# Another element order for the gate weights, and who makes the second one-hots and the score splits beside them

## What is computed

```python
def peer_ffn(h, w_q, keys, u_tab, v_tab):
    q = (h @ w_q).reshape(bsz, s, PK_HEADS, PK_DIM)
    s1 = einsum('bshd,hnd->bshn', q[..., :PK_HALF], keys[:, 0])
    s2 = einsum('bshd,hnd->bshn', q[..., PK_HALF:], keys[:, 1])
    v1, i1 = top_k(s1, 16)
    v2, i2 = top_k(s2, 16)
    cand = v1[..., :, None] + v2[..., None, :]
    best, c = top_k(cand, 16)
    e1 = take(i1, c // 16)
    e2 = take(i2, c % 16)
    expert = e1 * 128 + e2
    gate = softmax(best)
    # every token: 8 heads x 16 experts of 128 x 128
    act = gelu(einsum('tkd,td->tk', u_tab[expert], h))
    return einsum('tk,tkd->td', gate * act, v_tab[expert])
```

## Time and profile before

| | before |
|---|---|
| runs | 1711.5, 1711.54, 1712.85 us |
| median | 1711.54 us |
| the profiled execution | 1711.12 us |
| its span in the trace | 1709.3 us |
| PE busy | 1696.2 us, 99% of the span |
| DVE busy | 1393.0 us, 81% |
| ACT, POOL busy | 743.2 us, 664.6 us |
| granted TensorE clock | 1.00 of full (2.4 GHz) throughout |

### The profile page before, as it was taken

How to read it: one execution, slowest core, us unless ns; L and a number is a source line. 1 busy time by engine, 2 the same in 40 slices (tenths; PEclk the granted TensorE clock), 3 DMA queues, 4 the chain that set the end, 5 groups by cost and what they waited for, 6 DMA issues and landing times.

```text
span 1709.3 us, 33793 instructions
## 1 busy us (share of the span) xinstructions
PE 1696.2 (99%) x12021; PEld 1500.9 (88%) x12021; DVE 1393.0 (81%) x2763; ACT 743.2 (43%) x1060; POOL 664.6 (39%) x555
## 2 busy tenths in 40 slices
PE   9999999999999999999999999999999999999998
PEld 6878888788888999999998888888888888888887
DVE  5379989566688999999996998887778888777886
ACT  5555545543333333477774433333333333333333
POOL 0000000010253666788783554443334444343440
PEclk9999999999999999999999999999999999999999
DMA  5221122253322555566669999999999999999982
GB/s 184 87 75 40 49 95 79 87 195 121 122 76 74 169 173 175 179 237 249 234 231 352 391 394 392 330 331 342 345 366 345 345 337 332 334 356 356 352 309 97
DMA packets 158288, 399.07 MB, mean 233 GB/s; under 512 B 12512, under 2 KB 78176, under 8 KB 156416
## 3 DMA queue, kind: packets, MB, share of 16 engines
q1 hardware_dynamic: 118496, 252.20, 42.0%
q0 software_dynamic: 39712, 145.77, 22.8%
HBM read 353.75 MB, written 44.04 MB: 233 GB/s over the span
## 4 chain that ended last, share of the span: by engine, by line
PE 95%; DVE 2%; ACT 1%; DMA 1%; issue 0%; DVEq 0%; ACTq 0%
PE unit L426 95%; DMA g_dram<-ge 0%; DVE oneh L2121 0%; PE unit L578 0%; ACT L1164 0%; DVE rs L1654 0%; DMA xin<-xT 0%; DVE yo L2262 0%; ACT ld L1164 0%; DVE cy L1979 0%; ACT aa L1164 0%; ACT wH L1164 0%; DVE wL L1635 0%; ACT k L1164 0%; ACT best L1164 0%
## 5 line engine op out<-in xcount | busy, mean ns | idle before, releaser
L426 PE MATMUL unit<-h2H,uH 128*128 128x384 f32 x1024 | 348.9, 341 | 0.2 <-ACTq L1491 0.2
L426 PE MATMUL unit<-h2L,uH 128*128 128x384 f32 x1024 | 343.7, 336 | 0.0
L2324 POOL DMA_INDIRECT ring<-u_tab,idx x128 | 189.4, 1480 | 219.2 <-DVE accs L2198 192.3
L426 PE MATMUL unit<-vH,aH 128*128 128x512 f32 x768 | 237.9, 391 | 0.6 <-DVE aL L2173 0.5
L426 PE MATMUL unit<-vH,aL 128*128 128x512 f32 x768 | 237.2, 390 | 0.0
L426 PE MATMUL unit<-vL,aH 128*128 128x512 f32 x768 | 237.2, 390 | 0.0
L2324 POOL DMA_INDIRECT ring<-v_tab,idx x128 | 150.3, 1174 | 214.5 <-DVE ring L2184 208.2
L426 PE MATMUL unit<-h2H,uL 128*128 128x384 f32 x1024 | 204.0, 336 | 0.0
L1164 ACT ACTIVATE ge<-unit 128x384 f32<-128x384 f32 x128 | 62.4, 488 | 322.7 <-PE unit L426 322.7
L426 PEld LDWEIGHTS unit<-h2H,uH 128*128 128x128 f32 x1024 | 192.6, 188 | 2.8 <-issue 0.4
L426 PEld LDWEIGHTS unit<-h2L,uH 128*128 128x128 f32 x1024 | 192.5, 188 | 2.4
(11 more groups left out here) (316 smaller groups left out, 3204.5 us busy)
## 6 DMA issues: line engine op xcount, KB each, us to landing
uraw<-uT SPq DMA_DIRECT2D x128, 512.0 KB, 7.1
vraw<-v_tab SPq DMA_DIRECT2D x128, 512.0 KB, 8.6
wraw<-wall SPq DMA_DIRECT2D x68, 512.0 KB, 3.7
w_dram<-wst SPq DMA_DIRECT2D x12, 2048.0 KB, 6.7
wg<-w_dram SPq DMA_DIRECT2D x31, 768.0 KB, 9.7
g_dram<-ge SPq DMA_DIRECT2D x64, 192.0 KB, 1.9
gl<-g_dram SPq DMA_DIRECT2D x32, 384.0 KB, 11.6
gate_dram<-gst POOLq DMA_DIRECT2D x16, 256.0 KB, 2.3
```

The costliest lines, as they stand in the source:

```text
L426: return pe.matmul(out, lhsT, rhs, start=start, stop=stop, skip_group_check=True)
L2324: pool.indirect_dma_start(out=ring[k][:, :], out_offset=None, in_=(u_tab, v_tab)[half], in_offset=bass.IndirectOffsetOnAxis(ap=idx[:, SR * ...
```

## The change

Three edits.

1. The gate weights get another order of elements: `w_dram` is [group of four e1, partition, token, e1 in the group], and so are `wst` and `wg`. ACT's copy writes runs of four elements. A `wst` store goes out in runs of 512 bytes (32 tokens x 4 e1), 32 of them a partition. A `wg` load is one run of 6 KB a partition. `weigh` reads `wg` with a step of four elements.
2. POOL makes no one-hots. DVE makes the four `oh2` of a batch by one TENSOR_TENSOR of 128x512, the constant row (repeated four times) against the four tokens' values (each repeated 128 times). `e2s`, `oh2_ready`, `pool_order` and `batch_begun` are gone.
3. The stage's `u_low` (blocks 40 to 64) are POOL's, once per `j`. DVE's last `u_low` ahead of the main loop, of block 65, stays where it was, with a wait for POOL's.

```diff
-    e2s = at("e2s", 186.75, [P, 2 * T_W])
...
-    wst = at("wst", 125, [P, 2, NK, T_W])
+    wst = at("wst", 125, [P, 2, NG, T_W, G])
-    wg = at("wg", 157, [P, 2, NTB, G, T_W])
+    wg = at("wg", 157, [P, 2, TD, G])
...
                         batch = 16 * i + 4 * j + b
-                        pe.wait_ge(oh2_ready, batch + 1)
                         pe.wait_ge(rh_ready, batch + 1)
                         pe.wait_ge(wst_ready, batch + 1)
...
-                sp.dma_start(wg[:, par], w_dram[:, :, bass.ds(q * G, G), :].rearrange("b p e t -> p b e t")
-                             ).then_inc(wg_loaded[par], 16)
+                src = w_dram[q] if isinstance(q, int) else w_dram[bass.ds(q, 1)].rearrange("q p t e -> p (q t) e")
+                sp.dma_start(wg[:, par], src).then_inc(wg_loaded[par], 16)
...
-                        sp.dma_start(w_dram[bass.ds(2 * i + b, 1)].rearrange("b p e t -> p (b e) t"),
-                                     wst[:, b, :, :]).then_inc(wst_stored[b], 16)
+                        sp.dma_start(w_dram[:, :, bass.ds(2 * T_W * i + T_W * b, T_W), :].rearrange(
+                            "q p t e -> p q t e"), wst[:, b]).then_inc(wst_stored[b], 16)
...
-                    fn(wst[:, j // 2, :, o:o + 4].rearrange("p e t -> p t e"),
-                       bank[6 + b % 2][:, :].rearrange("p (t e) -> p t e", t=4), ACT.Copy).then_inc(wst_ready, 1)
+                    fn(wst[:, j // 2, :, o:o + 4, :].rearrange("p q t e -> p t q e"),
+                       bank[6 + b % 2][:, :].rearrange("p (t q e) -> p t q e", t=4, e=G), ACT.Copy).then_inc(wst_ready, 1)
...
-            dve.wait_ge(ul_ready, PRE_T)
-            u_low(PRE_T, 0)
...
                         for k in range(4):
                             tok = bass.ds(2 * T_W * i + 16 * j + 4 * b + k, 1)
-                            ins = tsc(rh[:, b, k, :], C(C_IOTA), et[:, 0, tok], et[:, 2, tok],
-                                      ALU.is_equal, ALU.mult)
-                            if k >= POOL_HOT:
-                                ins = tsc(oh2[:, b, k, :], C(C_IOTA), et[:, 1, tok], None, ALU.is_equal)
-                        ins.then_inc(rh_ready, 1)
-                        if b == 2:
-                            u_low(PRE_T + 4 * i + j + 1, (j + 1) % 4)
+                            tsc(rh[:, b, k, :], C(C_IOTA), et[:, 0, tok], et[:, 2, tok], ALU.is_equal, ALU.mult)
+                        four = et[:, 1, bass.ds(2 * T_W * i + 16 * j + 4 * b, 4)]
+                        tt(oh2[:, b, :, :], C(C_IOTA).unsqueeze(1).broadcast_to([P, 4, P]),
+                           four.unsqueeze(2).broadcast_to([P, 4, P]), ALU.is_equal).then_inc(rh_ready, 1)
...
-                tt(af[:, g % 2, :].rearrange("p (b t) -> p b t", t=T_W), src.rearrange("p (b t) -> p b t", t=T_W),
-                   wg[:, par, :, g, :], ALU.mult).then_inc(act_ready, 1)
+                tt(af[:, g % 2, :], src, wg[:, par, :, g], ALU.mult).then_inc(act_ready, 1)
...
+            dve.wait_ge(ul_ready, NPRE + 1)
             u_low(NPRE + 1, 1)
...
             with pool.Fori(0, PRE_T // 4) as i:
                 for j in range(4):
                     u_low(4 * i + j, j)
-            wait_taken(pool, "e2T")
+            u_low(PRE_T, 0)
             pool.wait_ge(idx_ready, 1)
...
-            for n in range(2):
-                hots(n)
-                fetch(n)
-            with pool.Fori(2, WI) as i:
-                hots(i)
+            fetch(0)
+            fetch(1)
+            with pool.Fori(0, WI) as i:
+                for j in range(4):
+                    u_low(PRE_T + 4 * i + j + 1, (j + 1) % 4)
```

More of the change, by code:

```diff
@@ L85 @@
 POOL_V = ()
-POOL_HOT = 2
 KB = 1024
@@ L321, in build @@
         wloh_ready, wlol_ready = sem("wloh_ready"), sem("wlol_ready")
-        dve_order, pool_order = sem("dve_order"), sem("pool_order")
+        dve_order = sem("dve_order")
         h_new, h_high, h_split = sem("h_new"), sem("h_high"), sem("h_split")
@@ L341, in build @@
         mix_ready, xr_loaded = sem("mix_ready"), sem("xr_loaded")
-        best_sub, best_exp, oh2_ready, batch_begun = (sem(n) for n in [
-            "best_sub", "best_exp", "oh2_ready", "batch_begun"])
+        best_sub, best_exp = sem("best_sub"), sem("best_exp")
         g_stored = [sem(f"g{i}_stored") for i in range(2)]
@@ L1112, in beside_w @@
                         if last:
-                            sp.dma_start(wg[:, 0, NTB - 2 + b], wst[:, b, 0:G, :]).then_inc(wg_loaded[0], 16)
-                        sp.dma_start(w_dram[bass.ds(2 * i + b, 1)].rearrange("b p e t -> p (b e) t"),
-                                     wst[:, b, :, :]).then_inc(wst_stored[b], 16)
+                            sp.dma_start(wg[:, 0, T_W * (NTB - 2 + b):T_W * (NTB - 1 + b), :], wst[:, b, 0]
+                                         ).then_inc(wg_loaded[0], 16)
+                        sp.dma_start(w_dram[:, :, bass.ds(2 * T_W * i + T_W * b, T_W), :].rearrange(
+                            "q p t e -> p q t e"), wst[:, b]).then_inc(wst_stored[b], 16)
                     store_g(n, j % 2)
@@ L1121, in first_wg @@
                     sp.wait_ge(wst_stored[i], 16 * (NTB // 2 - 1))
-                sp.dma_start(wg[:, 0, 0:NTB - 2], w_dram[0:NTB - 2, :, 0:G, :].rearrange("b p e t -> p b e t")
-                             ).then_inc(wg_loaded[0], 16)
+                sp.dma_start(wg[:, 0, 0:T_W * (NTB - 2), :], w_dram[0, :, 0:T_W * (NTB - 2), :]).then_inc(wg_loaded[0], 16)
                 sp.wait_ge(wst_stored[0], 16 * NTB // 2)
@@ L2331, in _ @@
                     u_low(4 * i + j, j)
-            wait_taken(pool, "e2T")
+            u_low(PRE_T, 0)
             pool.wait_ge(idx_ready, 1)
-            def hots(i):
-                pool.tensor_copy(e2s[:, :], et[:, 1, bass.ds(2 * T_W * i, 2 * T_W)]).then_inc(pool_order, 1)
-                pool.wait_ge(pool_order, i + 1)
-                for j in range(4):
-                    for b in range(4):
-                        pool.wait_ge(wmm_done, 16 * i + 4 * j + b + 1)
-                        pool.sem_inc(batch_begun, 1)
-                        for k in range(POOL_HOT):
-                            tok = 16 * j + 4 * b + k
-                            ins = pool.tensor_scalar(oh2[:, b, k, :], C(C_IOTA), e2s[:, tok:tok + 1], None,
-                                                     ALU.is_equal)
-                        ins.then_inc(oh2_ready, 1)
-                pool.wait_ge(oh2_ready, 16 * i + 16)
-            for n in range(2):
-                hots(n)
-                fetch(n)
-            with pool.Fori(2, WI) as i:
-                hots(i)
+            wait_filled(pool, "e1T")
+            wait_filled(pool, "e2T")
+            fetch(0)
+            fetch(1)
+            with pool.Fori(0, WI) as i:
+                for j in range(4):
+                    u_low(PRE_T + 4 * i + j + 1, (j + 1) % 4)
             def v_low(q, g):
@@ L2466 @@
         args[name] = nc.dram_tensor(name, a.shape, mybir.dt.from_np(a.dtype), kind="ExternalInput").ap()
-    args["w_dram"] = nc.dram_tensor("w_dram", (NTB, P, NK, T_W), F32, kind="Internal").ap()
+    args["w_dram"] = nc.dram_tensor("w_dram", (NG, P, TD, G), F32, kind="Internal").ap()
     args["g_dram"] = nc.dram_tensor("g_dram", (NPRE, P, TD), F32, kind="Internal").ap()
```

## The result

| | before | after |
|---|---|---|
| median | 1711.52 us | 1740.37 us |
| lowest and highest of 4 | 1710.86 to 1712.85 | 1739.88 to 1741.35 |
| ratio, 95% interval | | 1.0167 [1.0155, 1.0179] |
| span of the profiled execution | 1709.3 us | 1738.1 us |
| PE busy | 1696.2 us | 1704.4 us |

The change made the kernel 1.7% slower, by 28.9 us; the forecast was 1734 us. The span grew by 28.8 us: 23.0 in the gate-weight stage, 4.6 in the hole, 0.9 behind it, and 0.3 ahead of the stage. In the traces of the other kernels the stage begins between 719.7 and 722.5 us (720.2 before), through differences ahead of anything that the edits touch. So the three stretches need not add up to the difference of two times: a trace can be off by up to 2.3 us for this alone.

A forecast was written before the change was run, and what follows sets the result against it. PE was taken to bound the kernel, with DVE becoming slower in the stage: 1711.1 + 20.1 (stage) + 2.3 (last store) - 0.4 (ACT's copy) + 0.7 (main loop) = 1733.8, so 1734 us against the median; range 1717 to 1750.

The forecast's parts named there:

- What bounds the kernel: Gate-weight stage: PE bounds it at 7.74 us a `j`; only DVE exceeding that could change the time.
- DVE's own work: Stage: four `rh` at 0.257 us plus one comparison at 0.60, 1.63 us a batch, 6.51 us a `j`.
- rival (c): Stage: the comparison's repeated operand costs 1.03 ns an element more, 50 us, 1785 us in all; 9%.
- What POOL's splits do: Stage: each POOL split stops DVE for 2.1 us, a `j` becomes 8.61 us, the stage grows by 20.1 us.
- Rival (a): Stage: only DVE's two-operand instruction is stopped, 1.6 us a split, stage +8.0 us, 1722 us; 13%.
- Rival (b): Stage: not slower if a split costs DVE under 1.23 us; PE stays the bound, 1711.5 to 1714 us; 13%.
- Rival (d): Stage: POOL's split comes too late for PE's low part, PE waits for `ul_ready`, 1740 us or so; 3%.
- ACT's copy: Stage: ACT's copy of 512 elements falls from 1116 ns to 0.59 us without its step.
- The last `wst` store: Behind the stage: the twelfth store takes 9 us instead of 6.7, delaying the Gelu store ACT awaits: +2.3 us (0 to +8).
- ACT's copy at the stage's end: End of the stage: only the last, shorter ACT copy counts, -0.4 us (between 0 and -0.5).
- The main loop: Main loop: stepped `weigh` takes up to 0.39 us more, mostly covered by PE; +0.7 us at the start (0 to +3).
- `wg` loads: Loads become one run a partition, are issued a group ahead and lie off the chain: nothing gained.

The follow-up runs named there:

- comparison alone: Kernel before with only the four one-hots of a batch made by one DVE comparison, splits on DVE, old element order: 1712.10 us, ratio 1.0000.
- Half a split: Kernel after, but POOL splits only the first half of each block in the stage, other low parts left out: 1718.31 us (one run).
- two splits: Kernel after, but POOL does each split of the stage twice, one behind the other, into the same buffer: 1792.63 us (one run).
- the new order alone: Kernel before with only the new element order of the gate weights: 1720.11 us, ratio 1.0047 to before.
- after, wait moved: Kernel after, but ACT waits for stored Gelu results only before the first Gelu overwriting one, not ahead of the main loop: 1732.85 us, ratio 1.0121 to before.

## Why the prediction came out as it did

The direction, the mechanism and the place were right. The forecast was 6.4 us low: 2.9 of it in the stage, 2.7 in the hole, 0.2 in the main loop, 0.3 ahead of the stage, and 0.3 between the trace and the median.

**What bounds the kernel.** Right. PE bounded the stage, and only DVE could become the new bound. In every kernel in which DVE's `j` stays at or under PE's 7.74 us the stage takes 184.5 us, to the tenth.

**DVE's own work.** Right. The `rh` follow each other at 0.256 us (0.257 predicted), an `oh` holds DVE for 0.602 us (0.60), a `j` is 6.51 us. That the comparison's repeated operand costs nothing, as read from `cand`, held; rival (c) is out, by "comparison alone" too.

**What POOL's splits do.** The mechanism was right, and so was its form: one `rh` a `j` of over 2 us, DVE in the chain, DVE busy all the time. Only PE's waits look otherwise: not one in nearly every batch, as the prediction has it, but one in each `j`, since between two stops DVE makes a batch in 1.63 us and PE needs 1.94. The size was 2.2 us a split, the upper of the two rows, where I took 2.1: the row of the stopped TENSOR_SCALAR (2.22) was the nearer one; it is `rh`, a TENSOR_SCALAR, that is stopped. A `j` took 8.71 us instead of 8.61; 24 x 0.1 = 2.4 us, and the stage grew by 23.0 instead of 20.1. The other 0.5 us is not traced. Half a split and two splits put the loss on a line: 1.05, 2.2 and 4.4 us.

The Trainium skill's "SBUF — State Buffer", section "SBUF: two separate sides", says that the two engines exclude each other for the whole instruction. The trace agrees with the exclusion and not with the whole: 2.2 us of a split recorded as 2.40. "Half a split" agrees that either engine can be the one that waits. The time by that rule, 1741 us, is nearer to the result than mine, but by an accident: it puts 27 us into the stage (measured 23.0) and nothing more into the hole than I did. For the one-input instruction of POOL, DVE ran in the middle of it, with an `oh` of two inputs at its full pace, which the rule does not lead one to expect.

**Rival (a)**, only the two-operand instruction is stopped, is out: in after every instruction stopped in the stage is an `rh`, and no `oh` takes more than 0.69 us. **Rival (b)** is out for this kernel, but its bound, 1.23 us, is borne out by half a split on the one side and a whole one on the other. **Rival (d)** is out: PE waits for `oh`, never for `uL`, and POOL waits 147.5 us for work.

**ACT's copy.** 0.59 us predicted, 0.598 measured.

**The last `wst` store** is the step that was mis-sized. I took 9 us for it in place of 6.7, and 2.3 us for the hole. For the eleven stores that nobody waits for, 9 us was right: their landings take 8.7 to 9.0. The twelfth is the only one that counts, and it took 11.3 us where before's twelfth took 6.9: +4.4. The Gelu store landed 1.8 us behind it instead of 1.1: +0.7. Against the 2.3 that is 5.1, 2.8 us too low. The stores' short runs also held SP's queue for 4.77 us at the Gelu store's issue, but that was over 5.1 us before the store ahead had landed, so nothing shows that it cost time. Why the twelfth takes longer than the others is open: it took 9.7 us in "half a split", and 13.3 in "the new order alone". The upper bound of 8 us for the term took the 5.1 in, and the 6.6 of the kernel with edit 1 alone.

**ACT's copy at the stage's end.** -0.4 us predicted, and -0.5 measured, in the time from the last matmul of gate weights to the last `wst` store (1.45 us instead of 1.95).

**The main loop.** I had +0.7 us, for a dearer `weigh`; it is +0.9, for another reason. The group of `weigh` in the whole span, beside that of the earlier trace rows:

```profile
L2159 DVE TENSOR_TENSOR af<-ge,wg 128x384 f32<-128x384 f32 x64 | 54.5, 852 | 44.8 <-ACT ge L1160 44.8
```

It takes 0.30 us more (554 to 852 ns), within the bounds of 0 to 0.39. Behind the second group PE covers it as predicted: from the third group on, before and after take the same 24.77 us a group. For this one term the Trainium skill's "Vector Engine (DVE) Microarchitecture Reference", section 5.2, was close, with an estimate of 0.26 us. All of the 0.9 us lies in the first two groups: the first `unit` took 5.75 us instead of 4.36, the first group 26.41 us instead of 25.16, the second 24.77 instead of 25.15. The cause is the low clock after the longer hole, 0.59 from 945 to 950 us; no step of mine had it. With the hole at 12.1 us ("after, wait moved") the first `unit` takes 4.12 us with the same dear `weigh`. In all six kernels with a hole of 17.8 us or more it takes 5.64 to 7.07 us, in the seven others 4.12 to 4.36.

**`wg` loads** gained nothing, as predicted: their median went from 9.7 to 7.4 us, and no piece of the chain is one of them.

## What to carry to other kernels

Before work is given to an idle POOL, look for a place in the trace where that very instruction on POOL meets one on DVE, and charge the loss to DVE: here the split took DVE 1.24 us when it did it itself and 2.20 us when POOL did it. Compare the sum with what the bounding engine leaves (7.74 us a `j`): half a split cost the stage nothing, a whole one 23 us. And when a store is changed into short runs, ask who waits for it and for the transfers behind it on the same queue, and price the one store that is waited for, not the median: here eleven took 8.8 us, and the twelfth 9.7 to 15.7.

## What the runs showed of the hardware beyond what was expected

- A DMA of 4096 runs of 512 bytes holds up its queue: the issue of the next one on SP took 4.77 us instead of 0.36. Nothing shows that this delayed the landing: the issue was over 5.1 us before the store ahead had landed. In the transfers themselves, the packets of 512 bytes took 29 ns each in the median, those of 16 KB 620 ns.
- Either engine can be the one that is held: half splits that began within 0.25 us of an `oh` took 1.56 to 1.88 us instead of 1.27 to 1.37, and the `oh` their usual 0.68.
- One engine holding another shows in the chain as "issue", and in the waits not at all (in the stage DVE has no wait for POOL); only the length of single instructions tells it, 2.567 us against 0.334.
- POOL's one-input instruction stops DVE in two bursts and lets it run in between, 1.3 us in all out of 2.83; the two-input one holds it in one piece, 2.2 us out of 2.40.
- A wait behind a store is worth more than its length: 5.7 us of hole removed gave 6.4 us in the trace (7.5 between the medians), as the granted clock is 0.59 for five microseconds behind it.
- Taking a wait away gave nothing in the kernel before, although the wait stood in the chain: behind it the loads of `vraw` were late, up to 18.71 us on their way.
